# A mixture of experts on one core: gather from two float32r parts, items in the order of their experts, w2 read in 16 KB rows

## The reference, cut to what matters

```
def hierarchical_moe(xn, rg_w, rg_b, re_w, re_b, w1, w3, w2):    # xn = rmsnorm(h, norm_ffn_g)
    t = xn.reshape(bsz * seq, d)
    g_top, g_idx = lax.top_k(softmax(t @ rg_w + rg_b), 1)         # 1 group of 4
    e_logits = (the chosen group's 8 logits of t @ re_w + re_b)
    e_top, e_idx = lax.top_k(softmax(e_logits), 2)                # 2 experts of 8
    e_w = e_top / sum(e_top) * g_top
    expert_id = g_idx * 8 + e_idx
    gate = sum(one_hot(expert_id, 32) * e_w[..., None], axis=1)
    h = silu(einsum('td,edf->tef', t, w1)) * einsum('td,edf->tef', t, w3)
    h = h * gate[:, :, None]
    y = einsum('tef,efd->td', h, w2)                              # w1, w3: 2048x512, w2: 512x2048 per expert
```

## Time and profile before

| | us |
|---|---|
| median of three runs | 1477.6 |
| the profiled execution, its own time | 1479.44 |
| its span | 1477.7 |
| first `up` of item 0 (mixture begins) | 496.25 |
| end of the span, counted from the start of item 32's `up` at 1427.69 | 50.0 |

### The profile page before, as it was taken

How to read it: one execution, slowest core, us unless ns; L and a number is a source line. 1 busy time by engine, 2 the same in 40 slices (tenths; PEclk the granted TensorE clock), 3 DMA queues, 4 the chain that set the end, 5 groups by cost and what they waited for, 6 DMA issues and landing times.

```text
span 1477.7 us, 20807 instructions
## 1 busy us (share of the span) xinstructions
PE 1391.8 (94%) x8310; PEld 795.1 (54%) x8310; DVE 542.4 (37%) x1056; ACT 378.2 (26%) x655; POOL 220.4 (15%) x205
## 2 busy tenths in 40 slices
PE   6999999998897799999999999999999999999996
PEld 5885688896686444543543444435434444354343
DVE  4898810424512622322323223223232232232325
ACT  3210058665555211111102111111021111110202
POOL 2000265676685100000000000000000000000000
PEclk9999999999998899999999999999999999999998
DMA  8433353434258599999999999999999999999993
GB/s 206 171 115 114 120 194 114 146 140 171 99 196 332 210 424 427 425 427 424 426 427 427 425 426 428 427 424 428 426 427 424 427 427 427 424 428 426 427 424 127
DMA packets 80682, 484.19 MB, mean 328 GB/s; under 512 B 17393, under 2 KB 17474, under 8 KB 46210
## 3 DMA queue, kind: packets, MB, share of 16 engines
q1 hardware_dynamic: 79842, 481.28, 79.8%
q10 hardware_dynamic: 672, 2.10, 0.4%
q0 software_dynamic: 128, 0.26, 0.1%
HBM read 481.53 MB, written 2.10 MB: 327 GB/s over the span
## 4 chain that ended last, share of the span: by engine, by line
PE 57%; DMA 21%; ACT 3%; DVE 3%; issue 1%; POOL 0%; POOLq 0%; DVEq 0%; ACTq 0%
PE ps L1762 22%; DMA ring<-in_expert_w_dram 21%; PE ps L1434 10%; PE ps L1780 9%; PE ps L1740 6%; PE ps L1770 3%; PE ps L1791 2%; PE ps L1792 1%; PE ps L1752 1%; ACT reg_t L809 1%; DVE reg_e L1095 0%; PE ps L1690 0%; PE ps L1598 0%; DVE reg_y L1059 0%; PE ps L1550 0%
## 5 line engine op out<-in xcount | busy, mean ns | idle before, releaser
L1762 PE MATMUL ps<-ring,reg_y 128*64 128x512 f32 x1056 | 240.1, 598 | 31.6 <-DMA ring<-in_expert_w_dram 31.6
L1762 PE MATMUL ps<-reg_e,reg_y 128*64 128x512 f32 x1056 | 234.5, 593 | 0.8 <-DVE reg_y L1295 0.8
L1780 PE MATMUL ps<-ring,reg_y 128*64 128x512 f32 x1056 | 233.5, 595 | 0.8 <-DVE reg_y L1310 0.8
L530 POOL TENSOR_TENSOR w_lo<-ring,w_hi 128x512 fp32r<-128x512 f32 x144 | 183.7, 1302 | 86.1 <-ACT w_hi L597 84.2
L1762 PEld LDWEIGHTS ps<-ring,reg_y 128*64 128x64 f32 x1056 | 70.6, 136 | 183.3 <-issue 128.8
L1316 DVE TENSOR_TENSOR y_lo_t<-ps,y_hi_t 64x512 fp32r<-64x512 f32 x132 | 90.9, 689 | 213.0 <-ACT y_hi_t L838 211.6
L838 ACT ACTIVATE y_hi_t<-ps 64x512 fp32r<-64x512 f32 x132 | 78.1, 592 | 335.0 <-PE ps L1780 332.6
L1762 PEld LDWEIGHTS ps<-reg_e,reg_y 128*64 128x64 f32 x1056 | 74.7, 137 | 154.6 <-issue 143.1
L1780 PEld LDWEIGHTS ps<-ring,reg_y 128*64 128x64 f32 x1056 | 72.8, 137 | 134.7 <-issue 132.0
L1325 DVE TENSOR_TENSOR reg_x<-ps,reg_x 128x512 f32<-128x512 f32 x136 | 87.7, 684 | 122.3 <-PE ps L1792 122.0
L1306 DVE TENSOR_SCALAR reg_y<-ps,lamv 128x512 f32<-128x512 f32 x33 | 24.8, 751 | 256.3 <-PE ps L1762 256.3
(11 more groups left out here) (363 smaller groups left out, 1557.7 us busy)
## 6 DMA issues: line engine op xcount, KB each, us to landing
ring<-in_expert_w_dram SPq DMA_DIRECT2D x132, 2048.0 KB, 22.4
reg_e<-in_expert_w_dram SPq DMA_DIRECT2D x66, 2048.0 KB, 23.6
ring<-in_w_in_dram SPq DMA_DIRECT2D x20, 2048.0 KB, 8.0
ring<-in_w_out_dram SPq DMA_DIRECT2D x8, 2048.0 KB, 7.9
reg_x<-in_x_dram SPq DMA_DIRECT2D x4, 1024.0 KB, 9.2
out_dram<-reg_x SPq DMA_DIRECT2D x4, 512.0 KB, 2.7
reg_e<-in_ssm_w_glu_dram ACTq DMA_DIRECT2D x1, 1024.0 KB, 7.5
reg_d<-in_final_norm_g_dram ACTq DMA_DIRECT2D x1, 1024.0 KB, 5.0
```

The lines of the kernel that those rows point to most:

```text
L530: G.tensor_tensor(w_lo[:, i % BUFS, :], unit(u % SLOTS_A)[:, c, :], w_hi[:, i % BUFS, :], ALU.subtract).then_inc(row_lo, 1)
L1762: last = M(psb[m][64 * i:64 * i + 64, :], xeT[:, cc, 64 * q:64 * q + 64], unit(s)[:, c, :], start=cc < 2, stop=cc >= DC - 2)
L1780: last = M(psb[3 + i // 2][64 * (i % 2):64 * (i % 2) + 64, :], hT[:, 2 * half + f, :], unit2(s)[:, f, 512 * i:512 * i + 512], start=half = ...
```

## The change

- **Two parts.** The parts of h are now `h_hi` (h rounded to float32r) and `h_lo` (the rest, in float32r), and they hold h as it is, not times the reciprocal root. ScalarE writes `h_hi` (`h_high(k)`, 512 columns of each token block, between the last steps of the output projection), VectorE writes `h_lo` (`h_low(k)`), and GpSimd has no part in it. `selS` is float32r too. A gather is 16 x 2 x 2 = 64 matmuls. The reciprocal root goes into the scales of `a1` (ScalarE, now with a scale per slot) and of `a3`, so `gates` sums two columns.
- **Order of items.** The number of items of each expert is computed first (`passes`), and items are numbered by expert: experts 0 to 16 have items 0 to 16, the rest of expert 16 is item 17, expert 17 has item 18, and so on. SyncE loads each expert once; the units of expert 17 wait on `slot_free` for the units of item 17. The tables of ids, positions and gates cover all 40 possible items (`item_tables`), and are built by VectorE in pair 0 after `v_hidden(0)`; the first two items use tables made ahead (`first_pair`, `first_gates`).
- **Landing.** TensorE no longer waits on a slot's own semaphore: GpSimd waits for it (`item_landed`) and counts up `e_in`, on which TensorE waits.
- **w2** is read with rows p x 4 + c, so that each partition's part of a unit is one run of 16 KB and not two of 8 KB. The hidden activations take the same order of rows: `a1` and `a3` are written by reading their PSUM bank with a stride of 4 columns.
- The gain of the last norm is loaded by SyncE after the experts, into the region of the tables.

```diff
-        w2_v = e_w2.rearrange("l e (h c p) n -> p (l e) h c n", h=2, p=P)
+        w2_v = e_w2.rearrange("l e (p h c) n -> p (l e) h c n", h=2, p=P)
...
-            with sp.Fori(0, NE) as e:
-                item(e, e)
+            item(0, 0)
             sp.wait_ge(rk_ready, 2)
-            extra = sp.value_load(n_extra[0:1, 0:1], min_val=0, max_val=EXTRA - 1)
-            with sp.If(extra > 0):
-                with sp.Fori(0, extra) as x_:
-                    item(x_ + NE, sp.value_load(ids[0:1, ds(x_, 1)], min_val=0, max_val=NE - 1))
+            with sp.Fori(1, NE) as e:
+                item(sp.value_load(c_int[0:1, ds(e, 1)], min_val=1, max_val=ITEMS - 1), e)
...
+            def item_landed(e):
+                for k in range(6):
+                    s = slot_of(k)
+                    base = 16 * (UNITS_A // SLOTS_A) if s < SLOTS_A else 0
+                    g.wait_ge(ring_in[s], e * 16 + base + 16)
+                    g.sem_inc(e_in, 1)
...
+            def h_high(k):
+                for b in range(TB):
+                    A.activation(h_hi[:, b, :, 32 * k:32 * k + 32], h_columns(b, k), cp).then_inc(hp_hi, 1)
...
-                A.activation(a1, psb[0][:, :], cp).then_inc(e_a1, 1)
+                a.wait_ge(e_gsev, i_ + 1)
+                A.activation(v3(a1, P), psb[0][:, :].rearrange("p (q f) -> p f q", f=EC), cp,
+                             scale=g_slot[:, q, 0:1]).then_inc(e_a1, 1)
...
+                o8 = [P, ITEMS, NE]
...
+                for src_t, dst_t in ((x_q, posx), (gat, gatx)):
+                    for b in range(TB):
+                        link(V.tensor_tensor(x_t, x_in_e, src_t[:, b, :].unsqueeze(1).broadcast_to(o8), ALU.mult))
+                        link(V.reduce_sum(dst_t[:, b, :], x_t, axis=AX))
...
-                    for part in (hi, mid, lo):
+                    for part in (h_hi, h_lo):
                         for b in range(TB):
-                            last = M(psb[bank][:, (c % 4) * P:(c % 4) * P + ns], part[:, b, c * P:(c + 1) * P],
-                                     selS[:, b, 0:ns // SLOT, :].rearrange("p q s -> p (q s)"), start=k == 0, stop=k == 5)
+                            last = M(psb[bank][:, (c % 4) * P:(c % 4) * P + ns], part[:, b, c, :],
+                                     selS[:, b, 0:ns // SLOT, :].rearrange("p q s -> p (q s)"), start=k == 0, stop=k == 3)
```

More of the change, by code:

```diff
@@ L316, in build @@
         rk_ready = sem("rk_ready")
+        hp_hi = sem("hp_hi")
+        hp_lo = sem("hp_lo")
+        id_r = sem("id_r")
+        e_in = sem("e_in")
         e_sel = sem("e_sel")
@@ L554, in _ @@
             lows(ROWS)
[L556 to L567, removed]
+            def item_landed(e):
[4 more added lines that the diff above has]
+                    g.sem_inc(e_in, 1)
+            item_landed(0)
+            g.wait_ge(rk_ready, 2)
+            item_landed(g.value_load(id_1[0:1, 0:1], min_val=0, max_val=NE - 1))
+            g.wait_ge(rk_ready, 3)
+            with g.Fori(2, ITEMS) as i_:
+                item_landed(g.value_load(ids[0:1, ds(i_, 1)], min_val=0, max_val=NE - 1))
         @block.scalar
@@ L798, in _ @@
             h_evac(5)
+            h_high(2)
             highs(rows_out(8))
@@ L1237, in extra_items @@
-                v.wait_ge(rk_ready, 2)
+                for src_t, dst_t in ((x_q, posx), (gat, gatx)):
+                    for b in range(TB):
+                        link(V.tensor_tensor(x_t, x_in_e, src_t[:, b, :].unsqueeze(1).broadcast_to(o8), ALU.mult))
+                        link(V.reduce_sum(dst_t[:, b, :], x_t, axis=AX))
+                V.scalar_tensor_tensor(posx, iota_s[:, 0:ITEMS].unsqueeze(1).broadcast_to([P, TB, ITEMS]), -float(SLOT),
+                                       posx, ALU.mult, ALU.add).then_inc(rk_ready, 1)
@@ L1239, in _ @@
+                v.wait_ge(rk_ready, 3)
+            first_pair()
             v.sem_inc(e_h, 1)
@@ L1345, in v_items @@
                 v_hidden(n0)
-                if not first:
+                if first:
+                    item_tables()
+                else:
                     v_add(i_ - 1, (6, 7))
@@ L1721, in landed, with gather @@
             def landed(n_, k):
-                s = slot_of(k)
-                base = 16 * (UNITS_A // SLOTS_A) if s < SLOTS_A else 0
-                pe.wait_ge(ring_in[s], n_ * 16 + base + 16)
-                return s
-            def gather(i_, ns, first=False):
+                pe.wait_ge(e_in, n_ * 6 + k + 1)
+                return slot_of(k)
+            def gather(i_, ns):
                 pe.wait_ge(e_sel, i_ + 1)
@@ L1731, in gather @@
                     bank = (0, 1, 5, 0)[c // 4]
-                    if first and c % 8 == 0:
-                        pe.wait_ge(h_lo, c // 8 + 1)
-                        pe.wait_ge(h_lo_v, c // 8 + 1)
                     if c == 12:
@@ L1833, in pe_items @@
                     down(n0 + 1)
-            gather(0, P, first=True)
+            pe.wait_ge(hp_lo, 4 * TB)
+            pe.wait_ge(id_r, 1)
+            gather(0, P)
             pe_items(0, 0, QE, first=True)
```

177 lines of the change are left out of this document (91 added, 86 removed).

## The result

The changed kernel takes 1487.7 us (median of 7 runs), the kernel before 1479.6 in the same session (7 runs). The ratio is 1.0055, with a 95% interval of 1.0043 to 1.0067: **slower by 0.55%**, where 1469 us, faster than before, had been forecast. The profiled execution has a span of 1486.0 us.

The account below looks back on a forecast made before the run. Transfers bound the kernel, with TensorE 3.07 us a pair behind; the change would make TensorE the bound: 492.0 + 53.0 + 4.3 + 15 x 55.95 + 28.8 + 50.0 + 2.0 = 1469.4, forecast 1469 us, range 1450 to 1486.

Parts of the forecast that it names:

- transfer-bound version: Whole kernel if transfers set the end: 1456 us, or 1454 with a fast gather and a shorter queue gap.
- The gather's size: Gather in each pair: 64 matmuls at 108 ns take 6.9 us, +1.55 us a pair over the old 5.36.
- The other +0.25: Rest of each pair: +0.1 us for `slots_to_rows` with two 4-byte loads, +0.15 for the strided `a3`.
- the sum of +1.8: Each pair on TensorE: +1.8 us in all from gather, `slots_to_rows` and strided `a3`; sixteen pairs give 28.8.
- The first, second and third rivals: Gather per matmul: 56 to 80 ns (1454 us, chance 0.13); 120 ns (1482, 0.22); 214 ns (1586, 0.10).
- the one on the clock: First gather: lower clock for 3.8 us (18 matmuls), other 46 take 5.0; 8.8 us, item 0 starting at 492.0.
- the tables' step: Pair 0: thirteen 1280-column VectorE instructions, 19.6 us, delay `a3`, stalling TensorE 4.3 us (0 to 6) before second `turn`.
- The fourth rival: Unseen gaps: emptied queue after expert 16, relay and tables add a few us each; 1474 to 1480, chance 0.05.
- The standstill at expert 16: Transfer queue after expert 16 stands still 9.9 us, some 11 with the time from issue to first data.
- the single reading: Transfers: 12 MB fewer save 29.5 us, less the 11 us queue standstill, so that path ends 18.5 us earlier.
- The last part: From the last item's first `up` to the end: 52.0 us, including 2.0 for an unused gather.
- the allowance for it: Before the selection: 1 us for the output projection, covering 0 to 3 us of `h_low` contention with GpSimd.

Follow-up runs that it names:

- e5: Changed kernel with the earlier bfloat16 gather (three parts, 96 products) and the thirteen table instructions taken apart: 1456.7 us, ratio 0.9856.
- e1: Changed kernel with the thirteen wide table instructions taken apart, no longer in one block before the second turn: 1474.1 us, ratio 0.9974.
- e4: Changed kernel with the earlier gather of three bfloat16 parts as the only edit, tables still in one block: 1460.1 us, ratio 0.9876.
- e3: Changed kernel with tables taken apart and extra unread 512-column products (sixteen before the routing wait, eight before the first gather): 1467.6 us, ratio 0.9927.
- e10: e5 plus unread 512-column products, sixteen before the routing wait and four before the first gather: 1456.3 us, ratio 0.9865.
- e11: e1 plus 128 unread products of the float32r gather's own shape ahead of the first gather: 1500.5 us, ratio 1.0158.
- e2: Changed kernel with unread 512-column products, sixteen before the routing wait and eight before the first gather: 1481.2 us, ratio 1.0015.

## Why the prediction was wrong, step by step

**Its view of the bounds was right.** The two bounds lie 3.07 us a pair apart, and what TensorE gets to do sixteen times over is taken from that: the steady pair came out at 57.75 us and without transfer waits, as forecast. The forecast for a transfer-bound version was 1456 (1454 where the gather is fast); e5 gives 1456.7.

**The gather's size was right.** 64 matmuls at 108 ns were forecast and 112 measured, +1.79 us a pair for +1.55. The other +0.25 came to almost nothing (the strided `a3` takes 751 ns, as unstrided), so that the sum of +1.8 holds because two small errors cancel; that the pair fits to the hundredth is luck. In the last gather each matmul has 64 columns and still takes 112 ns (7.15 us would be the 64 at that rate; two take 0.22 in the timeline below), so the load sets the pace, not the columns. The weight load has a median of 192 ns in this kernel (its mean of 209 takes in the gathers at the lower clock), against 100 for the bfloat16 one. The first, second and third rivals are out by their own prices of 56, 120 and 214 ns.

**The step that failed is the one on the clock.** "So 3.8 us at 216 ns are 18 matmuls, the other 46 take 5.0": I carried over from rows 8 that the clock comes back after 3.8 us, as if that were a property of time alone. It was one of the bfloat16 gather. With float32r all 64 ran at 217 ns: 13.90 us and not 8.8. The same error stands unseen in the tables' step: "Stall: 4.3 us" was right in its size (3.6), but it was costed as a pause alone. Behind a pause TensorE's clock is down, and what follows here is half a `turn` and the gather, which do not bring it back: the 3.6 us of pause cost 12.8 (e1). Without them the change would have been the faster one (0.9974), even with its slow first gather.

The fourth rival had the gain shrink "to nothing" by gaps of a few us each. Its size (1474 to 1480) and its chance of 0.05 were too small, and its mechanism isn't the one either: the stall on the tables was shorter than in the sum, TensorE's waits on the relay add up to 2.1 us between 560 and 1440 us, and the emptied queue never shows in the chain. It is the clock behind the gaps that costs. The result lies 1.7 us beyond the upper end of the range, 1486.

The Trainium skill, page "TensorE: Matmul & The Clock Gate", section "Weight-path perf modes — Fast Weight Load (FWL) and DoubleRow", left open on which side float32r stands. The rows decide for this kernel: float32r loads in 192 ns at the full clock, like float32 (191), and not like bfloat16 (100).

**Smaller terms.** Thirteen wide instructions at 1.49 us: as forecast. The standstill at expert 16 is 14.9 us in e5 for the forecast 11, so the single reading saved 14.4 us where transfers bound the end, for 18.5. w2's longer rows were taken at nothing, with a bound of 0.05 us a unit (64 units, 3.2 us): they give 4.1. These two nearly cancel, and the 1456 came out better than its parts. A third part pays too: of the 22.4 us by which e5 beats the kernel before, 14.4 + 4.1 leave 3.9, and item 0's first `up` starts at 490.89 in e5 for 496.25, with the parts of h made earlier (4.2 was forecast for this). No run takes this part alone. The last part grew by 1.8 us over the forecast; the clock falls inside the last gather, which adds 1.3 us to it (8.49 for 7.15), and stays at 0.50 up to 1472, over the first matmuls behind it. Timeline of TensorE there, and two stretches, changed kernel:

```profile
1465.08 0.39 PE L1760 MATMUL ps<-selS,h_lo 128*128 128x64 f32 x2
1465.30 0.60 PE L1760 MATMUL ps<-selS,h_hi 128*128 128x64 f32 x2
1465.71 0.61 PE L1760 MATMUL ps<-selS,h_lo 128*128 128x64 f32 x2
...
1463.00:1465.00 2.00, 2.00 (x21) 2.00 (x20) 0.86 (x3) 0.00 (x0) 0.00 (x0) 1.00 0.00 0
1465.00:1468.00 3.00, 3.00 (x19) 2.94 (x18) 0.42 (x1) 0.00 (x0) 0.00 (x0) 0.55 0.03 5
```

h's parts beside GpSimd's splitting of the weights: `h_low` takes 3.0 us for its two instructions where GpSimd is at work, and 1.93 where it is not.

```profile
451.61 3.00 DVE L1148 TENSOR_TENSOR h_lo<-reg_x,h_hi 128x512 fp32r<-128x512 f32 x2 [4.82 <-ACT h_hi L784]
...
471.96 1.93 DVE L1148 TENSOR_TENSOR h_lo<-reg_x,h_hi 128x512 fp32r<-128x512 f32 x2 [1.08 <-ACT h_hi L784]
```

That is the contention which the Trainium skill's page "SBUF — State Buffer" names in "Who interferes with whom"; the allowance for it held, since the selection was on time (481.6 for 482.3).

**The parts of the change, by single edits.** Single reading: 14.4 us gained where transfers bound the end. w2's rows: 4.1 gained. The float32r gather: 26.7 us lost (e4). How that splits is an estimate from the traces of the changed kernel and e4: 13.0 us by the first two gathers (13.90 - 7.22 and 13.65 - 6.61), 3.3 more by the slower `up` and `down` behind them (8.54 - 7.09 and 8.77 - 6.92), and the rest, some 10, because TensorE's path is longer otherwise; e3 and e10, whose first gathers both have extra products ahead, differ by 11.3 us. The tables in one block: 12.8 lost with that gather, 3.5 without it (e4 to e5, whose intervals overlap).

## What to carry to other kernels

Fewer matmuls are not less work when their pace is set by loading 128 columns of 4-byte weights (64 of them took 7.15 us, 96 in bfloat16 5.36); count a gather by its loads. A pause on TensorE can cost its own length and then whatever follows at the lower clock, so ask what kind of matmul stands behind each pause: in these runs products of 512 columns and the bfloat16 gather brought the clock back, and a run of float32r loads with 128 columns each did not. When an edit takes the engine that was second over the first, the slack that hid all its small stalls is gone, and each of them shows in full at the end.

## What the runs showed of the hardware that I had not expected

- 192 float32r products of 128 columns in a row, 41.2 us without a gap, stayed at a granted clock of 0.50 (e11). The same products keep a clock of 1.00 in the steady loop, where they come 64 at a time between products of 512 columns.
- With 64 columns a matmul, the clock fell from 1.00 to 0.50 within such a run, with no pause before it: the change in pace at 1465.3 above. It did so in the last gather of all six kernels with the float32r gather (8.45 to 10.38 us for the 64, where 7.15 is the full clock). With 128 columns no such fall was seen inside a gather in the steady pairs, but in e2 the clock fell in the 0.78 us behind one. Whether the load's share or the columns decide was not taken apart.
- float32r and float32 load 128x128 weights in the same time (191 to 193 ns a record), 112 ns from matmul to matmul in the float32r gather and 108 in the float32 `turn`; bfloat16 loads in 98 to 100 ns, 56 ns from matmul to matmul.
- Transfers in runs of 16 KB moved 428 GB/s, with a third of the units in 8 KB runs 426.
